# Conditioning of features 0 to 511 in two rounds of 256 columns, with the first weight loads between them

## The reference, cut to what matters

```python
mod_ctx = (jax.nn.silu(c_ctx) @ w_ada[l] + b_ada[l])[None, None, :]
mod_lat = (jax.nn.silu(c) @ w_ada[l] + b_ada[l])[:, None, :]
...
sh1, sc1, gt1, sh2, sc2, gt2, sh3, sc3, gt3 = jnp.split(mod, N_MOD, axis=-1)
h = _rmsnorm(x, norm_ffn1) * (1 + sc1) + sh1
x = x + 0.5 * gt1 * _swiglu(h, w_ffn1_in, w_ffn1_out)
h = _rmsnorm(x, norm_mix) * (1 + sc2) + sh2
m, s_f, s_b = _mixer(h, w_mix_in, ...)
x = x + gt2 * m
h = _rmsnorm(x, norm_ffn2) * (1 + sc3) + sh3
x = x + 0.5 * gt3 * _swiglu(h, w_ffn2_in, w_ffn2_out)
```

## Time and profile before

| | us |
|---|---|
| median of 3 runs | 1303.25 (1301.76 to 1304.09) |
| profiled execution | 1302.81 |
| its span, first to last instruction | 1301.0 |
| TensorE busy | 1280.5 (98%) |
| VectorE busy | 927.6 (71%) |
| ScalarE busy | 550.7 (42%) |
| mean granted TensorE clock | 0.998 of full |

### The profile page before, as it was taken

How to read it: one execution, slowest core, us unless ns; L and a number is a source line. 1 busy time by engine, 2 the same in 40 slices (tenths; PEclk the granted TensorE clock), 3 DMA queues, 4 the chain that set the end, 5 groups by cost and what they waited for, 6 DMA issues and landing times.

```text
span 1301.0 us, 23108 instructions
## 1 busy us (share of the span) xinstructions
PE 1280.5 (98%) x8917; PEld 1227.4 (94%) x8917; DVE 927.6 (71%) x1534; ACT 550.7 (42%) x916; POOL 88.6 (7%) x71
## 2 busy tenths in 40 slices
PE   8999999999999999999999899999999999999997
PEld 7889999999999999999999899999999999988886
DVE  5668878787887864666798867547988887771424
ACT  6514544345532235663323554337444443551223
POOL 0000000000000000001313663000000000000000
PEclk9999999999999999999999999999999999999999
DMA  9871423322576733212544552242243423274222
GB/s 371 297 269 32 121 66 97 88 73 71 150 219 191 219 95 94 80 51 86 169 152 100 145 156 82 65 70 77 66 125 88 142 82 97 64 184 106 68 81 97
DMA packets 228132, 158.84 MB, mean 122 GB/s; under 512 B 45613, under 2 KB 203862, under 8 KB 227030
## 3 DMA queue, kind: packets, MB, share of 16 engines
q1 hardware_dynamic: 226436, 156.95, 40.7%
q10 hardware_dynamic: 1618, 0.81, 0.2%
HBM read 143.18 MB, written 14.56 MB: 121 GB/s over the span
## 4 chain that ended last, share of the span: by engine, by line
PE 87%; DVE 7%; ACT 2%; DMA 2%; issue 1%; another core or an unknown queue 1%; SPq 0%; ACTq 0%; DVEq 0%
PE ps L992 32%; PE ps L799 29%; PE ps L1437 12%; PE ps L1388 3%; PE ps L922 1%; DVE w_lo L2049 1%; DMA w_raw<-in_w_ffn_in 1%; PE ps L1164 1%; PE ps L1374 1%; DVE sub_tmp L2573 1%; PE ps L1151 1%; ACT w_hi L1473 1%; PE ps L867 1%; PE ps L1267 1%; PE ps L1274 1%
## 5 line engine op out<-in xcount | busy, mean ns | idle before, releaser
L1473 ACT ACTIVATE w_hi<-w_raw 128x1024 fp32r<-128x1024 f32 (+1 forms) x101 | 105.1, 1041 | 330.7 <-PE ps L799 170.8
L2049 DVE TENSOR_TENSOR w_lo<-w_raw,w_hi 128x1024 fp32r<-128x1024 f32 (+1 forms) x101 | 121.6, 1205 | 130.1 <-ACT w_hi L1473 128.0
L799 PE MATMUL ps<-h_hi,w_hi 128*128 128x320 f32 x736 | 173.1, 316 | 3.1 <-DVE w_lo L2049 3.0
L799 PE MATMUL ps<-h_lo,w_hi 128*128 128x320 f32 x736 | 169.5, 311 | 0.0
L799 PE MATMUL ps<-h_hi,w_lo 128*128 128x320 f32 x736 | 169.2, 311 | 0.0
L799 PEld LDWEIGHTS ps<-h_hi,w_hi 128*128 128x128 f32 x736 | 123.2, 189 | 7.9 <-issue 7.7
L992 PE MATMUL ps<-T_hi,S_hi 128*128 128x320 f32 x408 | 126.0, 309 | 0.0
L992 PE MATMUL ps<-T_hi,S_lo 128*128 128x320 f32 x408 | 126.0, 309 | 0.0
L992 PE MATMUL ps<-T_lo,S_hi 128*128 128x320 f32 x408 | 125.9, 309 | 0.0
L799 PEld LDWEIGHTS ps<-h_hi,w_lo 128*128 128x128 f32 x736 | 124.7, 189 | 0.0
L799 PEld LDWEIGHTS ps<-h_lo,w_hi 128*128 128x128 f32 x736 | 124.3, 189 | 0.0
(11 more groups left out here) (382 smaller groups left out, 2898.1 us busy)
## 6 DMA issues: line engine op xcount, KB each, us to landing
w_raw<-in_w_ffn_in SPq DMA_DIRECT2D x50, 512.0 KB, 4.6
cw_raw<-in_w_ada SPq DMA_DIRECT2D x40, 512.0 KB, 4.4
w_more<-in_w_ffn_in SPq DMA_DIRECT2D x34, 512.0 KB, 4.9
ada_w<-in_w_ada SPq DMA_DIRECT2D x16, 1024.0 KB, 8.7
w_raw<-in_w_ffn_out SPq DMA_DIRECT2D x30, 512.0 KB, 3.7
w_raw<-in_w_mix_in SPq DMA_DIRECT2D x28, 512.0 KB, 3.8
w_raw<-in_w_ffn_out SPq DMA_DIRECT2D x16, 448.0 KB, 4.0
w_raw<-in_w_mix_out SPq DMA_DIRECT2D x8, 512.0 KB, 3.9
```

Source lines behind the costliest of these rows:

```text
L799: last = pe.matmul(to[a_slot][b], w, m[:, k0 + k, part[b]], start=start and k == 0 and n == 0, stop=stop and k == kt - 1 and n == 2)
L1473: nc.scalar.activation(w_hi[:, slot, 0:kt * P], w_raw[:, slot, 0:kt * P], ACT.Copy).then_inc(hi_ready, 1)
L2049: nc.vector.tensor_tensor(w_lo[:, slot, 0:kt * P], w_raw[:, slot, 0:kt * P], w_hi[:, slot, 0:kt * P].bitcast(F32), ALU.subtract).then_inc( ...
```

## The change

The scale columns of features 0 to 511 are loaded and conditioned in two pieces of 256 columns by all 8 row blocks (`load_eighth`, `eighth_step`), where there were two pieces of 4 row blocks by 512 columns. One such step is complete in itself and gives the gains of two feature tiles; before, two steps gave those of four. The weight loads of the first two units stand between the two pieces on SP. There is one more turn, copy and set of gains, so the counts of the later ones move up by one. In `first_pair` the second row halves of tiles 0 and 1 move from behind `spread` to the places around the second piece's step and turn. The square root of the norms on ScalarE and `invert(0)` on VectorE keep their places behind tile 3.

```diff
             for j in range(2):
-                load_quarter(j, j, D)
+            load_eighth(0, D)
             for u in range(2):
                 load_w(u, u, w_in_v[0][:, :, u * FF:u * FF + P], KD, wait=False)
+            load_eighth(1, D + 256)
             for j in range(2):
                 load_quarter(2 + j, j, D + 512)
...
+            def eighth_step(n):
+                pe.wait_ge(ada_in[n], 16)
+                for k in range(KD):
+                    for g in range(2):
+                        at = 256 * k + g * P
+                        last = pe.matmul(adap[32 * g:32 * g + 32, 0:P], ccol[:, k, :], ada_w[:, n, at:at + P],
+                                         start=k == 0, stop=k == KD - 1)
+                last.then_inc(ada_mm, 1)
...
             pe.wait_ge(vec_rdy, 3)
-            for j in range(2):
-                quarter_step(j, j)
-            ada_turn(0, 1)
+            eighth_step(0)
+            ada_turn(0, 1, used=64)
             stir(6, 2 * P)
...
                 first(0, (0,))
                 first(1, (0,))
+                pe.wait_ge(x_ev, 2 * NC)
+                tile(0, 1, (0,))
+                eighth_step(1)
+                tile(1, 1, (0,))
                 pe.wait_ge(lo_ready, 2)
                 first(0, (1,))
+                ada_turn(1, 1, used=64)
                 first(1, (1,))
+                tile(0, 1, (1,))
+                tile(1, 1, (1,))
                 quarter_step(2, 0)
                 first(2)
                 quarter_step(3, 1)
                 first(3, (0,))
-                ada_turn(1, 1)
+                ada_turn(2, 1)
                 first(3, (1,))
-                pe.wait_ge(x_ev, 2 * NC)
                 spread(0)
-                tile(0, 1)
-                tile(1, 1)
                 first(4)
...
-                act.wait_ge(gain_rdy, 1 + k // 4 if m == 0 else 3 + m)
+                act.wait_ge(gain_rdy, min(1 + k // 2, 3) if m == 0 else 4 + m)
...
             for u in range(2):
                 split_hi(u, u, KD, 0, first=True)
+                if u == 1:
+                    ada_out(1, P, used=64)
                 for k in range(2 * u, 2 * u + 2):
                     gained_hi(0, k)
...
             for u in range(2):
                 split_lo(u, u, KD)
+                if u == 1:
+                    first_gains(1)
                 for k in range(2 * u, 2 * u + 2):
                     gained_lo(0, k)
             invert(0)
-            first_gains(1)
+            first_gains(2)
```

More of the change, by code:

```diff
@@ L889, in quarter_step, with ada_turn @@
                 last.then_inc(ada_mm, 1)
-            def ada_turn(n, blocks, src=ada_r):
+            def ada_turn(n, blocks, src=ada_r, used=P):
                 pe.wait_ge(ada_row, n + 1)
@@ L896, in ada_turn @@
                 for b in range(blocks):
-                    last = pe.transpose(adat[:, b * P:b * P + P], src[:, b * P:b * P + P], ident[:, :])
+                    last = pe.transpose(adat[:, b * P:b * P + used], src[0:used, b * P:b * P + P], ident[0:used, 0:used])
                 last.then_inc(ada_tr, 1)
@@ L1062, in _ @@
             turn_rows = lambda n: ada_turn(n, 2, cw_r)
[L1063 to L1065 removed]
+            behind = {2: lambda: column_rows(1), 3: lambda: turn_rows(6), 4: lambda: column_rows(2),
+                      5: lambda: (turn_rows(7), column_rows(3)), 6: lambda: (turn_rows(8), column_rows(4)),
+                      7: lambda: turn_rows(9)}
             swiglu_out(U_F1O, A_F1O, 0, g2_hi, g2_lo, banks_free(0), lambda j: behind[j]() if j in behind else None)
@@ L1510, in square, with ada_out @@
                 nc.scalar.activation(to[:, t0:t1], x[:, k, t0:t1], ACT.Square).then_inc(sq_rdy, 1)
-            def ada_out(n, width, dst=ada_r):
-                act.wait_ge(ada_mm, (2, 4, 8, 16, 17, 18, 19, 20, 21)[n])
+            def ada_out(n, width, dst=ada_r, used=P):
+                act.wait_ge(ada_mm, (1, 2, 4, 8, 16, 17, 18, 19, 20, 21)[n])
                 if n > 0:
                     act.wait_ge(ada_tr, n)
-                nc.scalar.activation(dst[:, 0:width], adap[:, 0:width], ACT.Copy).then_inc(ada_row, 1)
+                nc.scalar.activation(dst[0:used, 0:width], adap[0:used, 0:width], ACT.Copy).then_inc(ada_row, 1)
             def root(m):
@@ L1536, in gained_hi @@
                 last.then_inc(hh_rdy, 1)
-            ada_out(0, P)
+            ada_out(0, P, used=64)
             for u in range(2):
                 split_hi(u, u, KD, 0, first=True)
+                if u == 1:
+                    ada_out(1, P, used=64)
                 for k in range(2 * u, 2 * u + 2):
@@ L2061, in _, with ada_cols @@
                     "p (k f) -> p k f", k=4)).then_inc(x_ev, 1)
-            def ada_cols(n, base, blocks):
+            def ada_cols(n, base, blocks, groups=4):
                 dve.wait_ge(ada_tr, n + 1)
@@ L2069, in ada_cols @@
                 for b in range(blocks):
-                    src = adat[:, b * P:b * P + P].rearrange("p (g i) -> p g i", i=32)
+                    src = adat[:, b * P:b * P + 32 * groups].rearrange("p (g i) -> p g i", i=32)
                     for i in range(2):
@@ L2073, in ada_cols @@
                         last = nc.vector.tensor_tensor(
-                            mod[:, bass.ds(lo, 4, blocks), i], src[:, :, i], bada[:, bass.ds(lo, 4, blocks)], ALU.add)
+                            mod[:, bass.ds(lo, groups, blocks), i], src[:, :, i], bada[:, bass.ds(lo, groups, blocks)], ALU.add)
                 last.then_inc(mod_rdy, 1)
@@ L2121, in first_gains @@
             def first_gains(n):
-                ada_cols(n, KD + 4 * n, 1)
+                k0, k1 = ((0, 2), (2, 4), (4, KD))[n]
+                ada_cols(n, KD + k0, 1, k1 - k0)
                 dve.wait_ge(mod_rdy, n + 1)
-                gains(0, 4 * n, 4 * n + 4).then_inc(gain_rdy, 1)
+                gains(0, k0, k1).then_inc(gain_rdy, 1)
                 dve.wait_ge(gain_rdy, n + 1)
```

44 lines of the change are left out of this document (23 added, 21 removed).

## The result

| | median us | runs | ratio to before, 95% |
|---|---|---|---|
| before | 1303.4 (1299.6 to 1306.6) | 21 | |
| changed | 1306.65 (1303.4 to 1309.6) | 21 | 1.0024 (1.0018 to 1.0031) |
| changed, once more | 1306.53 (1303.9 to 1310.8) | 12 | 1.0028 (1.0016 to 1.0039) |

Each ratio is to runs of the kernel before that were made beside it; those of the second series have a median of 1303.09 us.

What follows compares the result with a forecast made beforehand. TensorE, carrying 87% of the chain, was taken as the bound. Start −1.02, extra step and turn +1.3, gaps +1.86 gave +2.1; the step-by-step +1.9 was kept: 1303.25 + 1.9 = 1305.1 us, range 1302.9 to 1307.4.

Steps and rivals of the forecast that it cites:

- A shift of the opening passes through: After 45 us TensorE's waits are mostly released by engines working on its own earlier output, so an opening shift reaches the end one for one.
- Before the first row half: One conditioning step of 16 matmuls replaces two, taking 1.01 us against 2.04; first turn at 16.14 instead of 17.16, gaining 1.02.
- Between the halves: From first row half at 19.60: second conditioning step done at 22.54, new turn at 23.54, without waiting for weights or copy.
- First and second new wait: TensorE idles 0.48 us before tile 2 and 2.0 before tile 4, each ready 3.04 us after its turn.
- The table load and the later transfers cost nothing: ScalarE's square root with table load is covered by the fourth step; later-issued conditioning loads still arrive before needed; no cost.
- Sum: Tile 4 starts at 32.27 instead of 30.35, +1.9 us; a second tally by terms gave +2.1.
- the clock falls in the gap: TensorE's 2.0 us idle from 30.24 drops its clock to 1.2 GHz, losing 2.2 us: 1307.4 in all; chance 0.09.
- my own sign: Listed sign of being wrong: a granted clock below 1.00 in the stretch 28 to 40 us.
- waits don't come: Both new gaps before tiles 2 and 4 vanish: 1302.7, or 1303.9 for half; chance 0.15 in part or whole.
- late transfers: Where opening loads run later than profiled, the old order pays and the new doesn't: 1304.7; chance 0.04.
- slow 1 KB rows: First conditioning load costs over 4.0 us per MB, so the first step starts late: +2.9, 1306.2; chance 0.04.

## Why the prediction was right in kind and short in size

- *A shift of the opening passes through.* Held for the first 200 us (+4.8 at 50 and at 200, +4.7 at 400 in the two profiles). Behind that waits that have nothing to do with the opening move it (+6.0 at 868, +3.7 from 880 on), and on the mean of the ten series the total is 1.0 us under the shift. One for one is right in kind; to 1 us it is not shown.
- *Before the first row half.* The term of the sum that was mis-sized. "Records 23.67 to 24.68 give 1.01 us for such a step": the new step has 16 matmuls too, but on two column groups, and took 1.87 to its end. It began 0.28 earlier than the first step of before, which lies within the scatter of that start, so the first turn came at 16.76, not 16.14, and won 0.40, not 1.02; counted from the first step it won 0.12. The transfers were there, as said.
- *Between the halves.* The same step a second time: done at 23.84, not 22.54; the turn at 24.91, not 23.54. The two together are 1.7 us, more than the 1.35 by which tile 4 was later than forecast; the earlier start hid the difference. Counted from the first step, tile 4 was forecast at 17.54 and came at 19.17, and at 17.49 with four column groups.
- *First and second new wait.* Held. Both are 3.04 us from the turn, the idle times 0.22 and 1.78 against 0.48 and 2.0. The delay being the same, the gaps differ by the work that TensorE had left behind each turn, which I had put 0.25 us too low.
- *The table load and the later transfers cost nothing.* Held; no wait for either in the profile.
- *Sum.* +1.9 at tile 4 was +3.27, and +1.53 with the slow steps taken out. Counted from the first step it is +3.55 and +1.87, so the rest of the sum, two new waits and all, came out within 0.1 us. With the clock's 0.5 on the mean, the 3.27 become 3.8 us, against 3.1 and 3.6 by the two ratios.
- *Rival: the clock falls in the gap.* I gave it 0.09 and a price of 2.2 us; it came in about a third of the executions and cost 1.5 each time. It is a term of the mean and not one of two outcomes. By my own sign, a clock below 1.00 between 28 and 40 us, the prediction was wrong here. The price was too high because I took a slow stretch of 4.4 us and it lasted 3.4. That the time stayed inside the range is in part luck: the upper end was drawn for the clock alone, and the slow steps, for which the sum had nothing, used up that room. My row against it, a stretch with a gap of 1.4 us that kept 2.4 GHz, was one sample of something that varies.
- *Rivals: waits don't come, late transfers, slow 1 KB rows.* None came. The 1 MB in 1 KB rows, issued at 3.23, landed 9.9 us later, at 13.1, before TensorE's step at 14.45.

## What to carry to other kernels

Read a duration from an instruction with the same place in the array, not only the same shape and count: halving the columns of a step halved its column groups, and so its matmuls no longer overlapped as before. Moving work to the front pays only if what it had covered stays covered; each turn here needs 3.04 us of other work behind it, and the change added a turn and took cover away from the other. Work whose result is needed only later belongs into time that is idle anyway, here the warm-up time ahead of the first row half. And count times from the start of the stage that was changed: a start that scatters by 0.66 us between executions otherwise reads as a gain or a loss.

## What the runs showed of the chip

- Conditioning matmuls on 32 output columns come in sets of as many records as there are column groups in turn: 7 ns apart within a set and about 109 ns from one set to the next, with two groups as with four. A step of 32 records so takes 1.87 us on two groups and 1.01 on four.
- The granted clock fell after an idle time of 1.78 us, with TensorE already busy again, and was at 1.2 GHz for 3.4 us (33.97 to 37.38 and 34.84 to 38.25). The same gap did so in two of three profiles, and by the mean clocks in about a third of the executions; four idle times of 1.71 to 1.86 us elsewhere had no fall behind them. In eleven of twelve profiles the clock stayed at 1.00 around 763 us; in that of the kernel with the twelve matmuls moved back TensorE had waited 2.22 us for GpSimd there, the longest of its idle times past 20 us in any of the profiles, and the clock fell at 764.04, with TensorE busy again for 0.5 us. TensorE's timeline and window of that kernel:

```profile
763.51 1.61 PE L1166 MATMUL ps<-Tc,NTb 128*128 128x128 f32 x8 [2.22 <-POOL NTb L2993]
```

```profile
764.00:767.50 3.50, 3.50 (x19) 3.50 (x19) 0.64 (x1) 1.85 (x3) 3.50 (x4) 0.51 0.58 105
```
